# Turning the residual unscaled: the RMS norm's reciprocal root moved behind the matmuls, its gain into the router weights and the gathered columns

## The reference

```python
h = rmsnorm(x, mix_norm_g);  x = x + concat([window_attention(h), pool(h)]) @ w_out
h = rmsnorm(x, xattn_norm_g); x = x + memory_cross_attention(h, rmsnorm(mem, mem_norm_g))
h = rmsnorm(x, ffn_norm_g);  x = x + hierarchical_moe(h)

def rmsnorm(x, g):  return x * rsqrt(mean(x * x) + EPS) * g
def hierarchical_moe(h):
    g_sel = argmax(h @ rg_w + rg_b)                      # one of 4 groups
    top_v, top_i = top_k((h @ re_w + re_b)[g_sel], 2)    # two of its 8 experts
    gate = softmax_prob(g_sel) * softmax(top_v)
    return sum(gate * ((silu(h @ w_gate[e]) * (h @ w_up[e])) @ w_down[e]) for e in chosen)
```

## Time and profile before

| | |
|---|---|
| runs of the kernel before | 1631.9, 1632.35, 1635.38 us; median 1632.35 |
| profiled execution | 1631.62 us; its span 1629.7 us |
| instructions in the span | 22070 |
| PE busy | 1517.8 us, 93% |
| DVE, ACT, POOL busy | 604.6, 365.5, 443.8 us (37, 22, 27%) |
| DMA | 471.93 MB, 290 GB/s over the span |
| granted TensorE clock, mean | 0.99 of full speed |

### The profile page before, as it was taken

One profiled execution on the slowest core, in us unless ns is written; L12 is line 12 of the kernel. 1 busy time (PEld: TensorE's weight loads), 2 busy tenths in 40 slices (PEclk: granted clock), 3 DMA queues, 4 the chain that ended last, 5 costly groups with the idle time before them and its releaser, 6 DMA issues.

```text
span 1629.7 us, 22070 instructions
## 1 busy us (share of the span) xinstructions
PE 1517.8 (93%) x6992; PEld 848.6 (52%) x6992; DVE 604.6 (37%) x746; ACT 365.5 (22%) x702; POOL 443.8 (27%) x2170
## 2 busy tenths in 40 slices
PE   7999999999999999899899899889999889989998
PEld 7787777758887466633243333323433333333333
DVE  6755656662324433523133223313313313312324
ACT  6422334352222244421011110110011101011011
POOL 4470035420000000044243332422423324233220
PEclk9999999999999999999999999999999999999999
DMA  8332222262324111599999999999999999999997
GB/s 311 104 104 77 78 78 75 84 193 96 103 78 147 59 54 50 233 369 428 427 427 429 427 429 428 429 429 427 429 428 428 430 428 429 428 428 430 428 424 298
DMA packets 88849, 471.93 MB, mean 290 GB/s; under 512 B 4642, under 2 KB 42716, under 8 KB 62556
## 3 DMA queue, kind: packets, MB, share of 16 engines
q1 hardware_dynamic: 88232, 470.84, 71.1%
q0 software_dynamic: 464, 0.35, 0.4%
q10 hardware_dynamic: 100, 0.03, 0.0%
HBM read 466.99 MB, written 4.21 MB: 289 GB/s over the span
## 4 chain that ended last, share of the span: by engine, by line
PE 70%; DMA 18%; DVE 6%; ACT 2%; issue 2%; SPq 1%; POOL 1%; ACTq 0%; DVEq 0%
PE ps L2310 22%; DMA weight_ring<-in_expert_w_up_dram 17%; PE ps L2010 11%; PE ps L1884 10%; PE ps L2340 7%; PE ps L2267 6%; PE ps L2063 3%; DVE residual L1692 2%; PE ps L1846 1%; PE ps L2404 1%; DMA residual<-in_x_dram 1%; PE ps L2126 1%; ACT weight_ring L922 1%; PE ps L1939 1%; PE ps L2123 1%
## 5 line engine op out<-in xcount | busy, mean ns | idle before, releaser
L2310 PE MATMUL ps<-weight_ring,proj_buffer 128*64 128x512 f32 x2040 | 474.3, 605 | 41.0 <-DMA weight_ring<-in_expert_w_up_dram 39.6
L722 POOL COPY proj_buffer<-transposed_acts (+1 forms) x1968 | 300.0, 215 | 616.7 <-ACT proj_buffer L1104 480.1
L2310 PEld LDWEIGHTS ps<-weight_ring,proj_buffer 128*64 128x64 f32 x2040 | 159.1, 139 | 344.5 <-issue 282.3
L1692 DVE TENSOR_TENSOR residual<-ps,residual 128x1024 f32<-128x1024 f32 x128 | 150.8, 1220 | 248.8 <-PE ps L2267 248.2
L2340 PE MATMUL ps<-weight_ring,proj_buffer 128*64 128x512 f32 x944 | 209.2, 595 | 15.6 <-issue 13.6
L1708 DVE SCALAR_TENSOR_TENSOR y_low<-ps,proj_buffer,y_high 64x1024 fp32r<-64x1024 f32 x60 | 77.0, 1283 | 231.4 <-ACT y_high L1115 230.4
L2340 PEld LDWEIGHTS ps<-weight_ring,proj_buffer 128*64 128x64 f32 x944 | 71.2, 137 | 136.1 <-issue 133.6
L1115 ACT ACTIVATE y_high<-ps,proj_buffer 64x1024 fp32r<-64x1024 f32 x60 | 66.5, 1109 | 285.0 <-PE ps L2340 284.3
L1884 PE MATMUL ps<-mix_high,w_in_high 128*128 128x512 f32 x288 | 117.3, 407 | 1.4 <-issue 1.4
L1104 ACT ACTIVATE proj_buffer<-ps 128x512 f32<-128x512 f32 x32 | 19.1, 598 | 438.0 <-PE ps L2310 438.0
L1884 PE MATMUL ps<-mix_high,w_in_low 128*128 128x512 f32 x288 | 112.3, 390 | 0.0
(11 more groups left out here) (330 smaller groups left out, 1812.7 us busy)
## 6 DMA issues: line engine op xcount, KB each, us to landing
weight_ring<-in_expert_w_down_dram SPq DMA_DIRECT2D x62, 2048.0 KB, 15.1
weight_ring<-in_expert_w_up_dram SPq DMA_DIRECT2D x61, 2048.0 KB, 20.3
weight_ring<-in_expert_w_gate_dram SPq DMA_DIRECT2D x60, 2048.0 KB, 15.9
weight_ring<-in_w_in_dram SPq DMA_DIRECT2D x18, 1024.0 KB, 5.6
weight_ring<-in_w_out_dram SPq DMA_DIRECT2D x16, 1024.0 KB, 5.0
weight_ring<-in_xkv_w_dram SPq DMA_DIRECT2D x8, 1024.0 KB, 7.5
residual<-in_x_dram SPq DMA_DIRECT2D x8, 1024.0 KB, 12.6
weight_ring<-in_expert_w_gate_dram SPq DMA_DIRECT2D x7, 1024.0 KB, 10.6
```

The costliest lines, as they stand in the source:

```text
L722: ins = g.tensor_copy(slots[:, :, j], H[:, :, ds(where[j], 1)].rearrange("p k n -> p (k n)"))
L1692: v.tensor_tensor(part, ps[:, bank:bank + 2, :].rearrange("p b n -> p (b n)"), part, ALU.add).then_inc(signal, 1)
L2310: ins = mm(ps[side * SLOTS:(side + 1) * SLOTS, 0, :], xsT[:, k, par * SLOTS:(par + 1) * SLOTS], gate_up_weights(e, u, kk), start=(k == 0), ...
```

## The change

The rows that TensorE turns are the residual itself: its weight operand reads `X[:, t, k::16]`, and nothing is scaled ahead of it. `hs` and `scaled_rows` go for this stage. The reciprocal root of a token is applied later instead, in two places: DVE multiplies each tile's logits by it as it adds the bias (`logits_scaled`, four instructions), and ACT multiplies the gate and up products of each block by it as it copies them out of PSUM (`scale=rs[...]`). `rs` is a table by slot and block, made as the gate table is, by the same matmuls with twice the columns (`Bw` has a second half, from `stat`). The norm's gain `gF` is multiplied into the router weights once, on DVE, behind the first tile's cross attention (`wr_scaled`), and into the token columns when they are gathered: POOL's and DVE's copies become multiplies, ACT's stay copies and DVE multiplies them afterwards in one instruction (`first_copied`). The shares of block 0 are now 18, 22 and 24; block 1's columns are all POOL's. The last tile's logits go to PSUM bank 6 (the others stay in 4). SP issues the half of expert 1's first gate unit ahead of expert 0's units.

```diff
@@ -57,8 +57,8 @@
 CUT = 3
-BY_ACT = 28
-BY_DVE = 20
+BY_ACT = 18
+BY_DVE = 22
 CLAMPED = "token numbers are sums of one-hot products over tokens, clamped to the last token where they are formed"
@@ -163,6 +163,7 @@
         all_ids = PB[0:1, 2048:2048 + NE * SLOTS].bitcast(I32)
+        rs = gT[:, 0:TCOL]
         ids = PB[0:NBLK, 9112:9112 + SLOTS].bitcast(I32)
@@ -504,6 +507,8 @@
                 sp.dma_start(xo_raw[n], xo_v[:, :, n * 512:(n + 1) * 512]).then_inc(landed[4 + 2 * n], 16)
+            sp.wait_ge(h_turned, 40)
+            sp.dma_start(second_gate, expert_unit(1, 0)[:, 0:CHK]).then_inc(half_gate_in[0], 16)
             for u in (1, 2, 0, 3, 4, 5):
@@ -516,8 +521,6 @@
-            sp.wait_ge(h_turned, 56)
-            sp.dma_start(second_gate, expert_unit(1, 0)[:, 0:CHK]).then_inc(half_gate_in[0], 16)
             sp.wait_ge(slot_onehot, 1)
@@ -719,19 +722,22 @@
                 for j in range(n):
-                    ins = g.tensor_copy(slots[:, :, j], H[:, :, ds(where[j], 1)].rearrange("p k n -> p (k n)"))
+                    ins = g.tensor_tensor(slots[:, :, j], H[:, :, ds(where[j], 1)].rearrange("p k n -> p (k n)"), gF[:, :], ALU.mult)
                 return ins
...
+            pool.wait_ge(small_in, 64)
             pool.wait_ge(first_ids, 1)
...
             copy_columns(first_row[0:1, BY_ACT + BY_DVE:SLOTS], xsT[:, :, BY_ACT + BY_DVE:SLOTS]).then_inc(first_rows[0], 1)
-            copy_columns(first_row[0:1, SLOTS + 32:2 * SLOTS], xsT[:, :, SLOTS + 32:2 * SLOTS]).then_inc(first_rows[1], 1)
+            for half in range(2, 4):
+                part = slice(half * 32, (half + 1) * 32)
+                copy_columns(first_row[0:1, part], xsT[:, :, part]).then_inc(first_rows[1], 1)
             pool.wait_ge(ids_ready, 1)
...
                    allow_small_or_imprecise_dtypes=True).then_inc(tramp_ready, 1)
-            pool.wait_ge(first_rows[0], 3)
+            pool.wait_ge(first_rows[0], 2)
             pool.wait_ge(first_rows[1], 2)
@@ -1043,18 +1049,6 @@
-            def scaled_rows(t):
-                act.wait_ge(rstd_done, 10 + t + 1)
-                if t < 2:
-                    act.wait_ge(h_turned, 40)
-                else:
-                    act.wait_ge(h_turned, 4 * (t + 9))
-                for m in range(4):
-                    k = 4 * ((m + 2) % 4)
-                    a.activation(hs[:, t % 2, :].rearrange("q (k p) -> q k p", p=P)[:, k:k + 4, :],
-                                 X[:, t, :].rearrange("q (p k) -> q k p", k=KD)[:, k:k + 4, :], ACT.Copy,
-                                 scale=stat[:, 2, 10 + t:11 + t]).then_inc(rows_ready, 1)
-
             query_squares(0)
@@ -1067,7 +1061,6 @@
             root_of(10)
-            scaled_rows(0)
             query_squares(3)
@@ -1076,10 +1069,8 @@
             root_of(11)
-            scaled_rows(1)
             cross_squares(2)
             root_of(12)
-            scaled_rows(2)
             act.wait_ge(tri_ready, 1)
@@ -1089,7 +1080,6 @@
             root_of(13)
-            scaled_rows(3)
@@ -1102,7 +1092,7 @@
                 a.activation(gu.rearrange("q (f p) -> q f p", p=P), ps[:, 0, :].rearrange("q (p f) -> q f p", f=KF),
-                             ACT.Copy).then_inc(gu_copied, 1)
+                             ACT.Copy, scale=rs[:, ds(b, 1)]).then_inc(gu_copied, 1)
                 act.wait_ge(gu_turned, b + 1)
@@ -1122,18 +1112,16 @@
             act.wait_ge(hT_ready, 56)
-            for par, first, last in ((0, 0, BY_ACT), (1, 0, 32)):
-                _, where = nc.values_load_multi_w_load_instructions(
-                    first_row[0:1, par * SLOTS + first:par * SLOTS + last], engines=(mybir.EngineType.Activation,), min_val=0, max_val=S - 1,
-                    skip_runtime_bounds_check_because=CLAMPED)
-                for j in range(first, last):
-                    ins = a.activation(xsT[:, :, par * SLOTS + j], H[:, :, ds(where[j - first], 1)].rearrange("p k n -> p (k n)"), ACT.Copy)
-                ins.then_inc(first_rows[par], 1)
+            _, where = nc.values_load_multi_w_load_instructions(
+                first_row[0:1, 0:BY_ACT], engines=(mybir.EngineType.Activation,), min_val=0, max_val=S - 1,
+                skip_runtime_bounds_check_because=CLAMPED)
+            for j in range(BY_ACT):
+                ins = a.activation(xsT[:, :, j], H[:, :, ds(where[j], 1)].rearrange("p k n -> p (k n)"), ACT.Copy)
+            ins.then_inc(first_copied, 1)
...
             a.activation(PB[:, 7676:7677], eps[:, 0:1], ACT.Silu)
-            gate_act(0)
             act.wait_ge(table_ready, 1)
-            down_act(0, 0)
+            block_act(0, 0)
             block_act(1, 1)
@@ -1502,8 +1490,14 @@
                     dve.wait_ge(h_turned, (10 + t) * 4 + m + 1)
-                    v.tensor_tensor(H[:, 4 * b:4 * b + 4, t * P:(t + 1) * P], ps[:, b, :].rearrange("p (k n) -> p k n", n=P),
-                                    wide(gF[:, 4 * b:4 * b + 4].unsqueeze(2), P, 4, P), ALU.mult).then_inc(hT_ready, 1)
+                    v.tensor_copy(H[:, 4 * b:4 * b + 4, t * P:(t + 1) * P],
+                                  ps[:, b, :].rearrange("p (k n) -> p k n", n=P)).then_inc(hT_ready, 1)
+
+            def logits_scaled(t):
+
+                dve.wait_ge(rstd_done, 10 + t + 1)
+                return v.scalar_tensor_tensor(out=L[:, t, 0:NCOL], in0=ps[:, 4 + 2 * (t // 3), t * NCOL:(t + 1) * NCOL],
+                                              scalar=stat[:, 2, 10 + t:11 + t], in1=rbias[:, :], op0=ALU.mult, op1=ALU.add)
@@ -1531,6 +1525,8 @@
             add_cross(0)
+            dve.wait_ge(router_in, 16 * (NG + 1))
+            v.tensor_tensor(wr, wr, wide(gF[:, :].unsqueeze(2), P, KD, NCOL), ALU.mult).then_inc(wr_scaled, 1)
             probs_out(1)
@@ -1573,10 +1569,13 @@
             r = rq
+            dve.wait_ge(logits_padded, 1)
+            for t in range(NT - 1):
+                if t == 0:
+                    dve.wait_ge(folded, NT - 1)
+                logits_scaled(t)
             dve.wait_ge(logits_done, 1)
-            dve.wait_ge(logits_padded, 1)
-            v.tensor_tensor(L[:, :, 0:NCOL], ps[:, 4, 0:NT * NCOL].rearrange("p (t c) -> p t c", c=NCOL),
-                            wide(rbias[:, :].unsqueeze(1), P, NT, NCOL), ALU.add).then_inc(logits_ready, 1)
+            logits_scaled(NT - 1).then_inc(logits_ready, 1)
             dve.wait_ge(logits_ready, 1)
@@ -1638,8 +1637,10 @@
             for j in range(BY_DVE):
-                ins = v.tensor_copy(xsT[:, :, BY_ACT + j], H[:, :, ds(where[j], 1)].rearrange("p k n -> p (k n)"))
-            ins.then_inc(first_rows[0], 1)
+                v.tensor_tensor(xsT[:, :, BY_ACT + j], H[:, :, ds(where[j], 1)].rearrange("p k n -> p (k n)"), gF[:, :], ALU.mult)
+            dve.wait_ge(first_copied, 1)
+            v.tensor_tensor(xsT[:, :, 0:BY_ACT], xsT[:, :, 0:BY_ACT], wide(gF[:, :].unsqueeze(2), P, KD, BY_ACT),
+                            ALU.mult).then_inc(first_rows[0], 1)
             link(v.scalar_tensor_tensor(out=r["inside"], in0=R, scalar=float(SLOTS),
@@ -1670,7 +1671,10 @@
             link(v.tensor_tensor(r["w"][:, 1], r["w"][:, 0], r["et"], ALU.mult))
-            v.tensor_tensor(r["Bw"], r["one"], wide(r["w"].rearrange("p k t -> p (k t)").unsqueeze(2), P, 2 * NT, TCOL),
+            v.tensor_tensor(r["Bw"][:, :, TCOL:2 * TCOL].rearrange("p (k t) c -> p k t c", k=2),
+                            r["one"].rearrange("p (k t) c -> p k t c", k=2),
+                            wide(stat[:, 2, 10:10 + NT].unsqueeze(1).unsqueeze(3), P, 2, NT, TCOL), ALU.mult)
+            v.tensor_tensor(r["Bw"][:, :, 0:TCOL], r["one"], wide(r["w"].rearrange("p k t -> p (k t)").unsqueeze(2), P, 2 * NT, TCOL),
                             ALU.mult).then_inc(gates_onehot, 1)
@@ -1680,6 +1684,8 @@
             dve.wait_ge(gates_done, 1)
+            for rows in (slice(0, SLOTS), slice(SLOTS, P)):
+                v.tensor_copy(rs[rows, :], ps[0:SLOTS, 5, TCOL:2 * TCOL])
             link(v.tensor_copy(gate[0:SLOTS, :], ps[0:SLOTS, 5, 0:TCOL]))
@@ -2132,17 +2138,18 @@
                     b = (m + 2) % 4
-                    pe.wait_ge(rows_ready, 4 * t + m + 1)
+                    pe.wait_ge(x_added, 16 + 4 * (t + 1))
                     if m == 2:
...
                     for k in range(4 * b, 4 * b + 4):
-                        ins = turn(ps[:, b, (k % 4) * P:(k % 4 + 1) * P], hs[:, t % 2, k * P:(k + 1) * P], ident[:, :])
+                        rows = X[:, t, :].rearrange("q (p k) -> q k p", k=KD)[:, k, :]
+                        ins = turn(ps[:, b, (k % 4) * P:(k % 4 + 1) * P], rows, ident[:, :])
                     ins.then_inc(h_turned, 1)
...
                 if t == 0:
-                    pe.wait_ge(router_in, 16 * (NG + 1))
+                    pe.wait_ge(wr_scaled, 1)
                     pe.wait_ge(bank_cleared, 1)
@@ -2156,7 +2163,7 @@
                 pe.wait_ge(halves_out, t + 1)
```

(16 more changed lines are left out.)

## The result

The changed kernel took 1637.76 us (median of 12 runs, 1635.82 to 1639.52) against 1633.0 (12 runs, 1630.32 to 1635.38). The ratio is 1.0029, its 95% interval 1.002 to 1.0038. So it is slower, inside the range and on the side that was forecast, but 4.2 us under the predicted 1642, and the sum behind 1642 was wrong in its largest term. Of the eleven executions of e1_dve20, further down, one took 8640.27 us and stands outside its ratio.

What follows compares the result with a forecast made beforehand. Compute-engine order sets the time until about 710 us, then the expert-weight stream. Terms 8.0 + 0 + 0.2 + 0 + 1.7 + 0.1 = +10.0 us on 1631.62 gave 1641.6, median 1642; range 1632 to 1647.

Steps and rivals of the forecast that it cites:

- The frame: Ahead of the expert-weight stream, a microsecond lost or gained comes out whole at the end; the stream's bytes are fixed.
- Turning the residual, +8.0: TensorE's 64 turns before the router logits: 64-byte-stride weight loads cost 0.14 us more a turn, +8.0 us (0 to +13).
- rival 1: TensorE's turns: the stride is free, leaving +2.0 us, 1634.4, or 1632.8 with POOL on time; chance 0.27.
- Scaled rows off ACT, 0: Router stretch: dropping ACT's 16 row-scaling instructions (17.4 us) gains 0 (0 to -0.3), since TensorE did not wait for them.
- Router weights, +0.2: DVE's one multiply scaling the router weights, 0.75 us, delays TensorE's start at 592.60 by +0.2 us (0 to +0.6).
- Columns of block 0, +1.7, by POOL: Gathering before block 0's products: POOL's 24 multiplies at 0.22 us each end last, +1.7 us (+0.1 to +4.8).
- rival 3: Router stretch: freed ACT or shorter copies close TensorE's gaps and its clock stays at 2.4 GHz, 1629 us; chance 0.08.
- Gate matmuls, +0.1: Gate table ahead of SP's transfer at 706.43: 16 matmuls move 100 columns instead of 50, +0.1 us (0 to +0.3).
- ACT's scaled copies, 0: Block 0: the scale on ACT's gate and up copies is hidden behind block 0's products, 0 us.
- Later blocks, 0: POOL's columns of block 1 and later blocks finish before their products, 0 us, block 2 with 5 us margin.
- the forecast's own sign: Test for block 0's products: start at about 702 us; a first start under 695 would make the prediction wrong.
- The second: Column gathering: POOL becomes the bound at 0.35 us a column, the stride being free, 1645 us; chance 0.07.

Runs made afterwards that it cites:

- e1_dve20: Changed kernel with block 0's column shares at ACT 20, DVE 20, POOL 24 instead of 18, 22, 24: 1635.51 us, ratio 1.0015.
- e4: Changed kernel, but TensorE turns contiguous unscaled rows copied by ACT, with SP's old queue order: 1637.59 us, ratio 1.0031.
- e10: Kernel before the change with block 0's column shares at ACT 24, DVE 20, POOL 20 instead of 28, 20, 16: 1631.04 us, ratio 0.9989.
- e3: Changed kernel with POOL's column multiplies made plain copies in all blocks, leaving out the norm's gain: 1638.36 us, ratio 1.0032.
- e9: Changed kernel with block 0's column shares at ACT 24, DVE 20, POOL 20 instead of 18, 22, 24: 1633.52 us, ratio 1.0006.
- e7: Changed kernel with block 0's column shares at ACT 20, DVE 22, POOL 22 instead of 18, 22, 24: 1642.11 us, ratio 1.0059.
- e8: Changed kernel with block 0's column shares at ACT 18, DVE 20, POOL 26 instead of 18, 22, 24: 1640.47 us, ratio 1.0055.

## Why the prediction was right in sign and wrong in its cause

- *The frame held*: what comes ahead of the stream moves the end by its own length. From block 1's first product on, every execution takes the same time within 1.7 us, and the stream's rate is the same.
- *Turning the residual, +8.0*: **this step failed**. The forecast was 0.14 us more a turn; the runs show 0.006, and 0.27 us for all turns and logits together (1.12 at 593.72 to 1.39 at 679.67). I took ACT's surcharge for a strided read as TensorE's. The load did get 0.056 us longer, within my bounds, but I let it add to the turn's period, and it overlaps. I also took 0.05 of the 0.111 us as the load's part of a turn, which no row shows. The lower bound, 0, which I gave as rival 1, is what happened. What the Trainium skill says in "SBUF — State Buffer", section "Door 1: The DMA port swizzle", of a cost for crossing 16-byte lines shows in the load's own length and not in the time of the turns.
- *Scaled rows off ACT, 0*: held; e4 puts unscaled copies back at no cost.
- *Router weights, +0.2*: +0.08. The multiply took 748 ns (0.75 forecast) and DVE's copy behind it started at 592.94, 0.41 later relative to the shift, of which ACT's part hid nearly all:

```profile
592.27 0.75 DVE L1529 TENSOR_TENSOR proj_buffer<-proj_buffer,ffn_gain_by_row 128x576 f32<-128x576 f32 x1
...
592.94 0.68 DVE L1459 COPY weight_ring<-ps 128x512 f32<-128x512 f32 x1
...
593.72 2.02 PE L2114 MATMUL ps<-weight_ring,memory_values 128*128 128x128 f32 x16 [0.79 <-ACT weight_ring L1043]
```

- *Columns of block 0, +1.7, by POOL*: **this step failed in the changed kernel by what it left out**, and was right for what it counted. It came to +3.24, by DVE. I took DVE's load of 22 numbers as 0.1 us longer than its load of 20, from the neighbouring rows; nothing in the trace of before had a load that starts off a multiple of four. Where the load is quick (e1), POOL is last and the term is +1.68. The price of 0.22 a column for two engines multiplying at once is borne out there (0.215); in the changed kernel POOL's columns took 0.184 each, while DVE stood waiting for most of them.
- *The clock*: rival 3 had it as a gain; it came as a loss of 1.66 us, behind an idle time of 4.34 us instead of 1.37. That the longer idle time alone made it is not shown: e10's execution lost as much (8.78 us for 32 products) behind 2.02 us.
- *Gate matmuls, +0.1*: +0.43 (15 of them in 1.28 us instead of 0.85). Twice the columns cost more than the bound of 0.3.
- *ACT's scaled copies, 0*: +0.14. They were to be hidden, but ACT's copy of block 0's last sums is on the path and takes 0.70 us instead of 0.60. The lines before:

```profile
705.49 0.85 PE ps L2237 x15
...
708.22 0.60 ACT proj_buffer L1104
```

- *Later blocks, 0*: held. POOL's block 2 columns, from 722.96 (716.42 in the earlier trace rows), at 0.184 each, end 13 us before block 2's products; e3 confirms it.

```profile
722.96 5.89 POOL L725 TENSOR_TENSOR proj_buffer<-transposed_acts,ffn_gain_by_row 128x16 f32 x32 [7.71 <-issue]
730.52 5.88 POOL L725 TENSOR_TENSOR proj_buffer<-transposed_acts,ffn_gain_by_row 128x16 f32 x32 [1.67 <-issue]
```

The measured terms make 0.27 + 0.08 + 3.24 + 1.66 + 0.43 + 0.14 = 5.82 us, against 5.85 read at block 1 (6.89 less the 1.04 of scatter); the medians differ by 4.8. That the measured time lies in the range is luck: an 8 us term was hardly there, and in its place came a load and a lower clock that were not foreseen. The same goes for the forecast's own sign, that no first start under 695 us would come: it came at 696.78, by DVE's load and not by the turns.

Of the rivals, the first was right on the stride, and its 1634.4 is near what the change cost with an aligned load and POOL last (e1: 1635.51). The second had the right place, the gathering, and the wrong engine.

## What to carry to other kernels

When a split of work between engines is shifted, look at where each share now begins, not only at how many items it has: in registers loaded from an SBUF row, a start off a multiple of four fp32-sized numbers cost about 0.235 us a number here instead of 0.06 to 0.08. Let such shares start at multiples of four; the shares alone moved the changed kernel from 1633.52 to 1642.11 us. And a longer weight load is not yet a longer matmul: price an overlapped step by the period of the pair, with a reading of both loads and matmuls, before a bound from another engine goes into the sum.

## What the runs showed of the hardware that was not expected

- Register loads of n numbers from an SBUF row. Start at a multiple of four numbers (16 bytes; the row itself begins at element 8768 of its buffer): 1.28 us for 16 (POOL), 1.61 for 20 (DVE), and 1.53 for 20, 1.77 for 24 and 2.03 for 32 (POOL). Off it: 4.74 for 20 and 5.18 for 22 (DVE), 5.13 for 22 and 6.00 for 26 (POOL), 2.5 and 2.8 for 11 (DVE). With an aligned start and a remainder of two: 2.08 for 22 (DVE). ACT, starting at 0, took 1.66 for 18 and 1.45 for 20.
- fp32 weight loads from a 64-byte stride: 196 ns instead of 140, with 0.117 us instead of 0.111 from turn to turn.
- TensorE's clock: an idle time of 4.34 us ahead of block 0 was followed by the lower level in the profile after, and so were 3.16 us (e9) and 2.02 us (e10); 2.79 us (e1) and 1.37 us (before) were not. The length of the gap alone does not decide. What TensorE did just before it differed too: its 36 idle matmuls took 5.45 us before and 5.86 in e1, but 5.83 after too, and 4.23 in e9 and e10. What decides is not shown.
- 128x16 multiplies of two SBUF operands on POOL: 0.184 us each while DVE waited, 0.215 and 0.26 beside DVE's work (e1; e7 and e8), 0.188 in e9, where DVE multiplied too.
